# One decoder step on one core: which queue issues the cache pages, and how the merge and the output projection are cut

## The reference

```python
z = xn @ w_in                          # 1024 -> projections of both branches and two gates ga, gb
oa = rwkv(...)                         # branch A, (tokens, 512)
ob = attend(q, k, v, log_f)            # branch B, (tokens, 512)
merged = sigmoid(ga) * (oa @ proj_a) + sigmoid(gb) * (ob @ proj_b)
h = h + merged @ w_out                 # (tokens, 1024)
# for a sample, attend reads 2048 past keys and values through a page table:
k_past = cache_k[page_table].reshape(8, 2048, 8, 64)      # 16 pages of 128 rows each, 8 heads
s = (q . keys) / 8 + c_q - c_k; softmax; probabilities @ values
h = h + hier_moe(rms_norm(h))          # 32 experts, 1024 -> 256 -> 1024, two for each token
```

## Time and profile before

| | |
|---|---|
| median of 3 runs | 935.49 us (933.38 to 940.15) |
| the profiled execution | 937.28 us, of which its span 935.7 us |
| PE busy | 791.2 us, 85% of the span |
| DVE, ACT, POOL busy | 354.2, 190.6, 149.0 us |
| DMA | 219.24 MB, mean 234 GB/s |
| the sample stage | about 440 to 662 us in the span |
| the moe stage | about 699 to 936 us |

### The profile page before, as it was taken

One profiled execution on the slowest core, in us unless ns is written; L12 is line 12 of the kernel. 1 busy time (PEld: TensorE's weight loads), 2 busy tenths in 40 slices (PEclk: granted clock), 3 DMA queues, 4 the chain that ended last, 5 costly groups with the idle time before them and its releaser, 6 DMA issues. The chain is left out here.

```text
span 935.7 us, 21030 instructions
## 1 busy us (share of the span) xinstructions
PE 791.2 (85%) x8857; PEld 491.1 (52%) x8857; DVE 354.2 (38%) x660; ACT 190.6 (20%) x427; POOL 149.0 (16%) x299
## 2 busy tenths in 40 slices
PE   3999899989679899877799777996959997899985
PEld 2445566656466657644366554665845443344421
DVE  3000533229742164255766365620253223232213
ACT  3000321216231211023312322221112110111112
POOL 8200120007040020030033423433000000000000
PEclk9999799988979879878799887998969998999998
DMA  8333141212320303247799995999645999999993
GB/s 323 125 126 140 48 148 48 72 66 77 116 54 20 108 9 95 66 141 263 234 380 417 393 372 210 364 407 375 263 180 226 423 424 422 423 417 424 423 425 122
DMA packets 54505, 219.24 MB, mean 234 GB/s; under 512 B 17887, under 2 KB 26378, under 8 KB 30858
## 3 DMA queue, kind: packets, MB, share of 16 engines
q1 hardware_dynamic: 47248, 186.23, 51.9%
q0 software_dynamic: 6512, 31.48, 8.7%
q10 hardware_dynamic: 650, 0.18, 0.1%
HBM read 211.29 MB, written 6.57 MB: 233 GB/s over the span
## 5 line engine op out<-in xcount | busy, mean ns | idle before, releaser
L229 PE MATMUL bank<-arena 128*128 128x320 f32 x256 | 82.7, 466 | 4.2 <-PEq L112 4.2
L208 POOL DMA_DIRECT2D arena<-in_cv x112 | 58.0, 518 | 127.0 <-PE bank L1869 97.3
L1459 DVE STREAM_TRANSPOSE arena<-arena 128x2048 f32<-128x2048 f32 x32 | 72.2, 2289 | 5.8 <-DMA arena<-in_ck 4.9
L505 PE MATMUL bank<-arena 128*128 128x336 f32 x224 | 71.2, 474 | 2.9 <-DVE arena L651 2.9
L2543 DVE TENSOR_TENSOR arena<-arena,bank 128x512 f32<-128x512 f32 x40 | 27.5, 688 | 108.3 <-PE bank L2331 105.3
L2354 PE MATMUL bank<-arena 128*32 128x512 f32 x512 | 62.9, 608 | 3.3 <-DMA arena<-in_w_exp 2.6
L484 PE MATMUL bank<-arena 128*128 128x512 f32 (+1 forms) x144 | 64.9, 614 | 0.0
L229 PEld LDWEIGHTS bank<-arena 128*128 128x128 f32 x256 | 48.6, 200 | 25.5 <-issue 9.4
L1869 PE MATMUL bank<-arena 128*16 128x128 f32 x1024 | 39.3, 322 | 22.7 <-issue 14.5
L505 PEld LDWEIGHTS bank<-arena 128*128 128x128 f32 x224 | 44.0, 201 | 26.1 <-issue 8.7
L1272 ACT ACTIVATE arena<-bank 128x384 f32<-128x384 f32 (+6 forms) x63 | 25.8, 444 | 124.1 <-PE bank L229 46.2
(11 more groups left out here) (477 smaller groups left out, 1122.9 us busy)
## 6 DMA issues: line engine op xcount, KB each, us to landing
arena<-in_w_exp SPq DMA_DIRECT2D x99, 1024.0 KB, 19.2
arena<-in_ck SPq DMA_DIRECT2D x128, 256.0 KB, 5.5
arena<-in_cv POOLq DMA_DIRECT2D x112, 256.0 KB, 7.6
arena<-in_w_gate SPq DMA_DIRECT2D x8, 1024.0 KB, 4.8
arena<-in_w_za SPq DMA_DIRECT2D x7, 1024.0 KB, 5.9
arena<-in_w_zb SPq DMA_DIRECT2D x6, 1024.0 KB, 15.1
arena<-in_cv SPq DMA_DIRECT2D x16, 256.0 KB, 3.5
arena<-in_w_proj SPq DMA_DIRECT2D x8, 512.0 KB, 9.0
```

The source lines that it names most:

```text
L208: eng.dma_start(tile[n:P:4, :], src[bass.ds(page, 1)].rearrange("a (p j) n -> (a p) (j n)", j=4))\
L229: mm = nc.tensor.matmul(bank[b][:, 0:TM], w[:, k, a, :], xnT[:, k, NMETA:T], start=(k == 0), stop=(k == KT - 1))
L505: mm = nc.tensor.matmul(bank[j % 2][:, 0:T], w[:, k, (j % 2) * P:(j % 2 + 1) * P], xnT[:, k, :], start=(k == 0), stop=(k == KT - 1))
L1459: return nc.vector.transpose(tile, tile)
```

## The change

It does six things. The values of samples 1 to 7 are issued by SP, between its key loads. The first load of gates stands at the end of `rwkv_post`, and the layout in DRAM is such that a partition's row is 10240 bytes in one piece. Two pieces of the merge stand between `scores(0)` and `scores(1)`, and the others are spread anew (`fill_no`). A piece `o` is now one pair of input blocks, 128 tokens and half the columns (512), so that there are 16 of two matmuls each where there were 8 of eight, and w_out comes in four plain loads of 1 MB. The addition of a piece `b` is done by VectorE. The last four pieces `o` stand before `weigh(7)` instead of behind it.

```diff
-        gates_dram = nc.dram_tensor("gates_dram", (2 * (DM // P), P, TM), f32, kind="Internal").ap()
+        gates_dram = nc.dram_tensor("gates_dram", (2, P, DM // P, TM), f32, kind="Internal").ap()
...
         def out_load(sp, c):
 
             s = out_slot[c]
-            src = A["w_out"].rearrange("n p (k c r) -> c n p k r", k=2, c=4)
-            dst = place[s].rearrange("p (n k r) -> p n k r", n=4, k=2)
-            for n in range(4):
-                sp.dma_start(dst[:, n], src[c, n]).then_inc(full[s], 16)
+            sp.dma_start(place[s], A["w_out"][c]).then_inc(full[s], 16)
...
                 for i in range(2):
                     sp.wait_ge(S(f"p_gt_out{i}"), 16 * (NPOST // 2))
+                sp.dma_start(gates, gates_dram[0]).then_inc(first_gates, 16)
...
-        FILL = [[("a", 0), ("a", 1), ("a", 2), ("a", 3)], [("a", 4), ("a", 5), ("a", 6), ("a", 7)],
-                [("b", 0), ("b", 1), ("b", 2), ("b", 3)], [("b", 4), ("b", 5), ("b", 6), ("b", 7)]]
-        FILL += [[("o", 2 * c), ("o", 2 * c + 1)] for c in range(4)]
-        fill_no = [sum(len(f) for f in FILL[:b]) for b in range(DB + 1)]
-        NFILL = fill_no[DB]
+        kinds = [("a", d) for d in range(ND)] + [("b", d) for d in range(ND)]
+        kinds += [("o", n) for n in range(4 * 2 * (NT - 1))]
+        fill_no = [0, 2, 5, 8, 11, 14, 18, 24, 28, len(kinds)]
+        NFILL = len(kinds)
...
-                gates_load(0)
+                def value_loads(b):
+                    for m in range(4):
+                        pages = [sp.value_load(pt_row[0:1, b * NPAGES + 4 * m + n:b * NPAGES + 4 * m + n + 1])
+                                 for n in range(4)]
+                        sp.wait_ge(S("pv_ps"), 4 * (b - 1) + m + 1)
+                        for n in range(4):
+                            page_load(sp, slot[4 + m], n, A["cv"], pages[n], vpool[m])
+
                 key_loads(2)
                 key_loads(3)
+                value_loads(1)
                 sp.wait_ge(S("fill_ps"), 4)
                 proj_load(sp, 1, 1)
                 for i in range(NT - 1):
                     sp.dma_start(tile_of(h2, i), A["xp"][i * P:(i + 1) * P, :]).then_inc(S("xr_in"), 16)
                 key_loads(4)
-                sp.wait_ge(S("fill_ps"), 8)
-                sp.wait_ge(S("fill_sb"), 8)
+                value_loads(2)
+                sp.wait_ge(S("fill_ps"), ND)
+                sp.wait_ge(S("fill_sb"), ND)
                 gates_load(1)
                 out_load(sp, 0)
+                key_loads(5)
+                value_loads(3)
                 out_load(sp, 1)
-                for b in range(5, DB):
-                    key_loads(b)
+                key_loads(6)
+                value_loads(4)
+                key_loads(7)
+                value_loads(5)
                 sp.wait_ge(S("sco_ps"), DB - 1)
-                for c in range(2, 4):
-                    out_load(sp, c)
+                out_load(sp, 2)
+                value_loads(6)
+                out_load(sp, 3)
                 for s in (2, 3):
                     ahead(sp, s)
+                value_loads(7)
...
-                    for m in range(4):
-                        pages = [pool.value_load(pt_row[0:1, b * NPAGES + 4 * m + n:b * NPAGES + 4 * m + n + 1])
-                                 for n in range(4)]
-                        pool.wait_ge(S("pv_ps"), 4 * (b - 1) + m + 1)
-                        for n in range(4):
-                            page_load(nc.gpsimd, slot[4 + m], n, A["cv"], pages[n], vpool[m])
-                    for f, (kind, d) in enumerate(FILL[b - 1]):
-                        if kind == "b":
-                            pool.wait_ge(S("fill_sb"), fill_no[b - 1] + f + 1)
-                            nc.gpsimd.tensor_tensor(mT[:, d, 0:SEQ], mT[:, d, 0:SEQ], btmp, add)\
-                                .then_inc(S("m_ready"), 1)
...
                 scores(0)
+                fills(0)
                 for b in range(DB):
                     if b < DB - 1:
                         scores(b + 1)
                     if b:
                         turn_out(b - 1)
                     turn_probs(b)
+                    if b == DB - 1:
+                        pe.wait_ge(S("pT_sb"), 4 * DB)
+                        pe.wait_ge(S("pn_sb"), DB)
+                        fills(DB)
                     weigh(b)
                     if b < DB - 1:
-                        for n in range(len(FILL[b])):
-                            fill(b, n)
-                fill(DB - 1, 0)
+                        fills(b + 1)
                 turn_out(DB - 1)
-                fill(DB - 1, 1)
```

More of the change, by code:

```diff
@@ L1714, in place_fills @@
                 return first_fill[s] + 64
-            return {8: 0, 9: 0, 10: 64, 15: 64, 16: 96, 17: 32}[s] if s not in range(11, 15) else kneed(7, s - 11)
+            return {8: 0, 9: 0, 10: 16, 15: 64, 16: 48, 17: 32}[s] if s not in range(11, 15) else kneed(7, s - 11)
         def ahead(sp, s):
@@ L1885, in turn_out, with fill @@
                         .then_inc(S("oT_ps"), 1)
-                def fill(b, n):
-                    kind, d = FILL[b][n]
-                    f = fill_no[b] + n
+                def fill(f):
+                    kind, d = kinds[f]
                     out = bank[5 + f % 2]
-                    if n >= 2:
+                    if f >= 2:
                         pe.wait_ge(S("fill_sb"), f - 1)
                     if kind == "o":
-                        c, i = divmod(d, 2)
+                        c, i, half = piece(d)
                         pe.wait_ge(*out_fill(c))
                         pe.wait_ge(S("m_ready"), ND)
-                        w = place[out_slot[c]].rearrange("p (k n) -> p k n", k=KT)
-                        for k in range(KT):
-                            mm = nc.tensor.matmul(out[:, 0:QTR], mT[:, k, i * P:(i + 1) * P], w[:, k, :],
-                                                  start=(k == 0), stop=(k == KT - 1))
+                        w = place[out_slot[c]].rearrange("p (k n) -> p k n", k=2)
+                        for k in range(2):
+                            mm = nc.tensor.matmul(out[:, :], mT[:, 2 * c + k, i * P:(i + 1) * P],
+                                                  w[:, k, half * HALF:(half + 1) * HALF], start=(k == 0), stop=(k == 1))
                     else:
@@ L1910, in fill, with fills @@
                     mm.then_inc(S("fill_ps"), 1)
+                def fills(n):
+                    for f in range(fill_no[n], fill_no[n + 1]):
+                        fill(f)
                 scores(0)
+                fills(0)
                 for b in range(DB):
@@ L2117, in fill_out, with fills_out @@
                     else:
-                        TT(btmp, out[:, 0:SEQ], gates[:, d, 0:SEQ], mult).then_inc(S("fill_sb"), 1)
+                        ch(TT(btmp, out[:, 0:SEQ], gates[:, d, 0:SEQ], mult))
+                        dve.sem_inc(S("fill_sb"), 1)
+                        ch(TT(mT[:, d, 0:SEQ], mT[:, d, 0:SEQ], btmp, add))
+                        dve.sem_inc(S("m_ready"), 1)
+                def fills_out(n):
+                    for f in range(fill_no[n], fill_no[n + 1]):
+                        fill_out(f)
                 for m in range(2):
@@ L2142, in _ @@
                         scale_out(b - 1)
-                        for n in range(len(FILL[b - 1])):
-                            fill_out(b - 1, n)
+                    fills_out(b)
                     if b < DB - 2:
@@ L2176, in logits @@
                     ch(nc.vector.tensor_copy(lg[:, i, :], bank[(0, 6, 4)[i]][:, 0:E_]))
-                for i in range(NT - 1):
-                    norm(i)
+                norm(0)
+                norm(1)
                 dve.wait_ge(S("sb_ps"), 1)
```

50 lines of the change are left out of this document (24 added, 26 removed).

## The result

| | before | changed kernel |
|---|---|---|
| median of the runs | 934.96 us (933.38 to 940.15, 4 runs) | 969.00 us (967.42 to 970.87, 4 runs) |
| span of the profiled run | 935.7 us | 969.1 us |
| mean granted TensorE clock | 0.905 | 0.889 |

The ratio is 1.0355, 95% interval 1.0308 to 1.0401: the change costs 34 us. The forecast was 951 us, range 941 to 960. The direction came as forecast, and so did the mechanism of most of the loss; the size was twice what was forecast, and some 6 us of it come from something that the forecast doesn't have.

What follows compares the result with a forecast made beforehand. moe's start bounds the end, and SP's serial tile issue at 3.83 us delays it: L1933 starts 15.5 us later, so 937.28 us profiled becomes 952.8, less 1.8 for the median: 951 us, range 941 to 960.

Steps and rivals of the forecast that it cites:

- The start of moe sets the end: Expert stream at the end: fixed length from moe's start, so a delay of moe's start moves the end by as much.
- SP's row of batches: Cache block: SP issues 11 key and value batches from 449.99 us, setting TensorE's pace; weigh(5) ends at 627.8 us.
- The gains of the other edits: Hidden pieces, additions on VectorE, waits of weigh(7): 18 us gained if SP's issue is no limit (first rival, chance 0.05).
- break-even of 3.48 us per tile: SP's tile issue: if a tile costs less than 3.48 us, the changed kernel is not slower.
- 3.83 us as the price of all tiles: SP's issue of one tile, four table reads and four DMAs, taken from the window at 530 us.
- row of 4.00: First eight key tiles on SP: 4.00 us each, the upper end of the tile price; 6 us more over the other 36.
- third rival: SP's queue also held by full DMA rings: 15 us more of stops, L1933 near 690 us, 963 us; chance 0.08.
- pieces ahead of weigh(7): Last pieces on TensorE moved before weigh(7): they cover its waits of 2.29, 2.91 and 1.71 us.
- expert slots: Loads ahead of moe: 12 of 18 slots filled by about 693 us, moe starts near 715 us; in time, no cost.
- clock's 2.3: Low TensorE clock at the end of weigh(5): 0.8 us for its last quarter, 1.5 for the first pieces behind it.
- forecast of 15.5 us: L1933, the first instruction of the serial stretch before moe, starts at 677.8 us, 15.5 us later than before.
- What was costed at nothing: Pieces between first scores, gates, additions, expert slots: no cost or gain; ScalarE waits 15 to 20 us for second gates, hidden.

Runs made afterwards that it cites:

- run 2: Kernel before, with only the values of samples 1 to 7 moved to SP at the changed kernel's places: 964.51 us, ratio 1.0364.
- run 1: Changed kernel with the values of samples 1 to 7 issued by GpSimd again, as before the change: 924.96 us, ratio 0.9897.
- run 4: Changed kernel with constant page numbers for the values instead of page table reads, same bytes and DMAs: 935.98 us, ratio 1.0038.
- run 5: Changed kernel with two of each value tile's four pages issued as two half-page DMAs, same bytes: 1001.21 us, ratio 1.0743.
- run 9: Changed kernel, values still on SP, with two of the last four pieces behind weigh(7), one ahead of turn_out(7), one behind it: 965.25 us, ratio 1.0369.
- run 10: Run 1 with two of the last four pieces behind weigh(7), and value tiles 2 and 3 of each sample on SP: 916.67 us, ratio 0.9849.
- run 11: Changed kernel with 4900 more semaphore increments on otherwise idle GpSimd, to load more code there: 1092.86 us, ratio 1.1736; misfired as a timing.

## Why the prediction was wrong

**The mechanism of the larger part was right.** The start of moe sets the end (moe lasts 235.5 and 236.4 us). SP's row of batches sets when TensorE gets through (run 2: the move alone delays proj_b by as much as the whole change). The gains of the other edits are swallowed (run 1: they are there once the values leave SP). The break-even of 3.48 us per tile held in run 4 (3.45, proj_b as before), and run 5 shows one for one above it.

**The step that failed most: the price of SP's row of batches.** I took 3.83 us as the price of all tiles and allowed 1.4 us for stops, those of the first eight tiles alone. From the first to the last issue of each, the ten runs of tiles to the end of sample 5's values took 164.1 us together, where 3.83 per tile gives 154.9: 9.2 us of stops where I had allowed 1.4. The reads and loads between them took 18.5 instead of 16.5. Together sample 5's values ended 9.3 us after the forecast. With its stops a tile took 4.04 us, (164.1 + 10 x 1.36) / 44, so the row of 4.00 in the earlier trace rows was the better mean. I had it as the upper end, and called the 3.83 steady because it was the window without a stop. The third rival had just this mechanism, 15 us of stops, and put L1933 near 690 us; measured 688.7. But its reason, full DMA queues, isn't borne out: with SP alone the stops are there, and when one of its 16 long issues began, only 1 to 4 DMAs (2.9 in the mean) were issued and not landed, where the other page issues had 3.4 in the mean and up to 10.

**The second: the clock behind weigh(7).** I looked for low clock only where TensorE waits. The price that I set there was right: the last quarter of weigh(5) at 1.91 us instead of 1.07 and the 24 matmul rows of the six pieces behind it in 12.52 instead of 24 x 0.45 = 10.8 make 2.6 us, against 2.3 forecast. Not in the sum was proj_b itself: from L1944 to moe 44.0 us instead of 37.8, 6.2 us. I costed the pieces ahead of weigh(7) by the waits that they cover, and never asked what follows weigh(7) once they are gone from there. Run 9 shows that with the clock right I would still have been wrong here: without the slow proj_b the late ln_rows cost the same time by themselves (44.6 us from proj_b to moe). So these 6.2 us have two causes, and either one is enough. I had named the DMAs that a moved step delays only for the expert slots, and ln_rows stand in the same queue behind the same values.

**The rest of the sum.** From the end of weigh(5) to L1944: forecast 50.0 with the clock's 2.3, measured 50.7. The end of weigh(5) against the last issue: 5.8 us against 4.9. moe 0.8 longer. So against the forecast of 15.5 us stand 9.3 for the batches, 6.2 for proj_b, 1.6 for the small steps on the way and 0.8 for moe: 33.4, the difference of the two spans.

**What was costed at nothing** was nothing. ScalarE's wait for the second gates was 19.55 us (15 to 20 forecast), scores(4) stood at 550.8 (553), and SP first asked for them at 568.8. Of the two waits for additions one stayed, hidden. The 18 slots were full in time.

**The rule of the Trainium skill**, "DMA: Bandwidth & Descriptors", section "Issuing engines are not separate DMA queues", that an issue is usually small relative to its DMA, doesn't hold for this kernel: a page costs SP 0.96 us and the DMA engines 0.62. Runs 4 and 5 vary the first with the second unchanged, and the time follows the first.

**Left open:** what stretches some of SP's issues, what in the order of matmuls lowers the clock, and why run 2's moe block is 5 us longer. Loading ln_rows ahead of the values in the changed kernel wasn't tried.

## What to carry to other kernels

Before two queues are merged, write out the row of one period: all issues with their register reads, against the time of the engine that they feed. As long as the row fits it is free (run 10: 23 us, in samples 24.4 to 25.0 us apart), and beyond that each microsecond counts in full; the mean DMA share (0.85 here) doesn't show it. Take the price of an issue from a long row with its stops in it, and not from the cleanest window, when over a hundred of them stand in a chain. And when work is moved off an engine or ahead of a step, ask what then follows that step directly, on the engine's clock and in the queue.

## What was not expected of the hardware

- **Long issues on SP.** 16 of 208 page issues took over 0.6 us instead of 0.472, 8.4 us more together. In the records 12 of these 16 (not all, as the expectation of run 11 has it) lie within 1 us of a packet of the instruction queue q8, which has only 20 packets in that time. In run 2 it is 9 of 9, in run 4 15 of 17, in run 5 13 of 16, in run 9 11 of 13, in run 10 9 of 10, in the kernel before 4 of 5. GpSimd's packets go on q14 (run 11). Whose q8's are, and whether they hold the issue or both have a cause in common, no run shows.
- **The clock falls on a busy TensorE.** It was granted 1.00 up to 688.7 us and 0.54 behind it, with 14.27 of the 16.5 us before and 13.29 of the 13.30 us behind busy. Whether proj_b runs slow depends on what stands between it and weigh(7): it did in five of five kernels with one order and in none of seven with another.
- **Counting on GpSimd is slow.** In run 11, 700 increments of a semaphore took 56.14 us, 80 ns each.
